# Pool and convolution-gate panels as seven block products, with weight sums made by DMA

## The chip, the cores and the metric

The kernel runs on one core of a Trainium2 chip. The metric is the device time of one launch in microseconds; it is compared as the median of several runs, and one more execution is recorded by the hardware profiler.

## The reference

The reference is one decoder block on 512 tokens of width 1024 in float32, with 256 memory tokens. Cut to what the change touches:

```python
h = rmsnorm(x, g_mix)
proj = h @ w_in                                   # 512 x 1024 @ 1024 x 6144
za, zb, zc, zg = jnp.split(proj, IN_SPLITS, axis=-1)
ya = chunked_spatial_gating(gelu(za)) @ w_branch_a
yb = short_gated_conv(zb, b_conv) @ w_branch_b    # gb * conv3(gc * xin)
yc = multiscale_pool(zc, c_wg, c_scale) @ w_branch_c
gates = jax.nn.sigmoid(zg.reshape(nb, s, 3, D_MODEL) + b_gate)
x = x + (gates[:,:,0]*ya + gates[:,:,1]*yb + gates[:,:,2]*yc) @ w_o
x = x + cross_attention(x, mem)                   # keys and values from rmsnorm(mem) @ w_xkv
x = x + swiglu_ffn(x)
```

A final RMSNorm follows. Two pieces of `proj`, each 512 columns wide, are the subject: `gb` (the gate that multiplies the convolution) and `zc` (the input of the pool).

## The kernel before

**Panels.** All weights come as panels of 128 partitions x 2048 float32 (1 MB), numbered in the order of use: V0 = 0 (values), K0 = 4 (keys), SV0 = 8, SU0 = 10, GC0 = 12, XI0 = 14, PC0 = 16 (pool, two panels), GB0 = 18 (convolution gate, two panels), GA0 = 20 (six times two gate panels and one branch panel), and then the output projection, the attention and the feed-forward part. SyncE (SP) loads panel n into slot n % 2 of `raw` as soon as the low part of panel n - 2 is made (`lo_ready`), in order, one queue.

**Splits.** Every float32 product is three matmuls (`mm3`, lines 1614 to 1616): high by high, high by low, low by high. For each panel ACT copies `raw` to a rounded high part (`split_hi`), and DVE subtracts it to get the low part (`split_lo`). Both are in-order engines and walk through a hand-written list of such steps, interleaved with the arithmetic of the stage.

**Full and seven-product panels.** `fm_panel` (line 1629) computes 256 output features for 512 tokens with 48 matmuls of 512 columns. The twelve gate panels from GA0 on use `gate_seven` (line 1794): the panel is cut into 2 x 2 blocks, and seven block products with sums of weight blocks (S1 to S4) and sums of token blocks (T1 to T4, `gth`/`gtl`) replace eight. It has 84 matmuls of 256 columns. Between its products ACT keeps partial results (`keep`: s1, s5, u2, u3 into `gsnap`), and DVE adds them at the end (`gate_add`). The weight sums are four DVE additions in `gate_prep` (line 1163), in place in `raw`; `gate_pair_hi` and `gate_prep_lo` then split the sums into high and low parts.

**The order around the change.** TensorE runs XI0 (two panels), sixteen transposes, PC0 and PC0+1, GB0 and GB0+1 as full panels, four pool products (three matmuls each), then GA0 and GA0+1 in seven products and the first branch panel. ACT copies the pool input to `zp`; DVE computes the running means from it (`pool_window`) and multiplies the convolution by the gate. POOL makes the weight sums of the feed-forward output, `fo_sums`, in DRAM with accumulating DMAs, beginning when `mixed` is reached; each step waits until the one before has landed.

**The first products.** `v_half(0)` computes two value panels whose pieces arrive one after the other; each step waits for the high and low parts of both operands. Ahead of it `WARM` = 14 products of ones run, 28 matmuls in the profile.

Of the kernel before, what the change touches and what calls it, by code (L numbers as in the profile page):

```python
# [28 lines left out]
P = 128  # L29
D = 1024  # L30
S = 512
# [12 lines left out]
NG = 12  # L44
# [7 lines left out]
WARM = 14  # L52
# [32 lines left out]
def build(nc, first_in, weights, fo_in, x_in, xt_in, memt_in, cols_in, sgu_in, wg_in, ln_g_in, ln_b_in, gf_in, out):  # L85
    base = -(-nc.sbuf_base // 32) * 32

    kv_store = nc.dram_tensor("kv_store", (4, P, KT * M), F32).ap()
    fo_sums = nc.dram_tensor("fo_sums", (NP, P, 4, S), F32).ap()
# [25 lines left out]
    gsnap = at("gsnap", 200, [2, S])  # L115
    hole = lambda t: t[:, 0:4, S // 2:S].rearrange("p k (b f) -> p b k f", b=2)
# [85 lines left out]
    with ExitStack() as ctx:  # L202
# [29 lines left out]
        def landing(n):  # L232
            return 16 * (n // SLOTS - K0 // SLOTS + 1)
# [46 lines left out]
        fo_made = sem("fo_made")  # L280
# [46 lines left out]
        def _(sp):  # L327
# [12 lines left out]
            with sp.Fori(K0 // 2 + 1, FO0 // 2) as i:  # L340
                for s in range(SLOTS):
                    sp.wait_ge(lo_ready, 2 * i + (s - 1))
                    sp.dma_start(raw[:, s, :], weights[2 * i + (s - 2)]).then_inc(landed[s], 16)
            for q in range(2 * NP + 1):
# [6 lines left out]
                if q == 0:  # L351
                    sp.wait_ge(fo_made, 16 * 3 * NP)
# [18 lines left out]
        def _(pool):  # L371
# [22 lines left out]

            pool.wait_ge(panel_done, K0 + 1)
# [14 lines left out]
            made = 0  # L410
            for step in range(NP + 2):
                if step < NP:
                    pool.dma_start(fo_sums[step], fo_in[step, :, 0:4 * S].rearrange("p (b c) -> p b c", b=4)).then_inc(fo_made, 16)
                    made += 16
                if 1 <= step <= NP:
                    q = step - 1
                    pool.dma_start(fo_sums[q, :, 1:4, :], fo_in[q, :, 3 * S:6 * S].rearrange("p (b c) -> p b c", b=3),
                                   accum_op=ALU.add).then_inc(fo_made, 16)
                    made += 16
                if step >= 2:  # L420
                    q = step - 2
                    pool.dma_start(fo_sums[q, :, 0:4:2, :], fo_sums[q, :, 1:4:2, :], accum_op=ALU.add).then_inc(fo_made, 16)
                    made += 16
                pool.wait_ge(fo_made, made)
# [29 lines left out]
        def _(act):  # L454
# [130 lines left out]
            split_hi(XI0 + 2)  # L585

            for g in range(BT):
                act.wait_ge(a_fm, g + 1)
                copy(acth[:, g, :], bank[4 + g][:]).then_inc(acth_ready, 1)
            def gate_sigmoid(h, j, t):  # L590
                b, half = h // 2, h % 2
                i = 4 * half + 2 * j + t
                act.wait_ge(gate_sum if t == 0 else up_sum, 2 * h + j + 1)
# [4 lines left out]
                nc.scalar.activation(sig[:, 2 * j + t, :], bank[2 * j + t][:], ACT.Sigmoid,  # L598
                                     bias=col(C_BG + 8 * b + i)).then_inc(low_read, 1)

            def gate_panel_of(h, j):

                return GA0 + 3 * h + j, 2 * h + j
# [9 lines left out]
            def gate_pair_hi(n, i, pair):  # L613
                act.wait_ge(s2_ready if pair == 0 else s4_ready, i + 1)
# [3 lines left out]
            def keep(i, j, which):  # L618

                left, right = bank[2 * j], bank[2 * j + 1]  # L620
                done, kept, dst, src = {
                    "s1": (p1_done, s1_kept, gsnap[:, 0, 0:Q], right[:, Q:S]),
                    "s5": (p5_done, s5_kept, gsnap[:, 1, Q:S], left[:, Q:S]),
                    "u2": (p6_done, u2_kept, gsnap[:, 0, Q:S], right[:, Q:S]),
                    "u3": (p7_done, u3_kept, gsnap[:, 1, 0:Q], right[:, Q:S])}[which]
                act.wait_ge(done, i + 1)
# [15 lines left out]
            for n in range(2):  # L642
                split_hi(PC0 + n + 1)
                if n:
                    pool_hi(0)
                    pool_hi(1)
                for t in range(2):
# [1504 lines left out]
```

## Time and profile before

| what | us |
|---|---|
| median of 3 runs (lowest, highest) | 884.63 (884.46, 885.09) |
| profiled execution | 884.56 |
| its span (first to last instruction) | 882.7 |
| TensorE busy | 874.2 |
| DVE busy | 649.0 |
| ACT busy | 420.0 |
| POOL busy | 78.4 |

The span is what the profiler's records cover; the profiled execution's own time is a little longer. Busy time counts each engine by itself, and matmuls overlap, so that their mean durations don't add up to their busy time; stages are read from the times at which they start. A weight panel's "us to landing" is counted from its issue on the queue.

### The profile page before, as it was taken

The numbers are of one execution on the slowest core, as the hardware profiler recorded it, in microseconds if no ns is written. First come the engines' busy times: TensorE is split into PE (matmuls) and PEld (weight loads), VectorE is DVE, ScalarE is ACT, GpSimd is POOL, SyncE is SP. The second block draws the span as 40 slices with busy tenths as digits, with TensorE's granted clock in tenths as the row PEclk, the third lists the DMA queues.
The fourth block names the chain that finished last, engine by engine and source line by source line (L and its number), as shares of the span: only waits on it lengthen the run. The fifth ranks groups of instructions, "written<-read, shape, count | busy, mean of one in ns | idle before, by whom it ended". The sixth has DMA issues, their size and how long they took to land.

```text
span 882.7 us, 13301 instructions
## 1 busy us (share of the span) xinstructions
PE 874.2 (99%) x5232; PEld 781.9 (89%) x5232; DVE 649.0 (74%) x825; ACT 420.0 (48%) x629; POOL 78.4 (9%) x89
## 2 busy tenths in 40 slices
PE   9999999999999999999999999999999999999997
PEld 7998888889999999988888888899999999988885
DVE  5684667688676687765456465898888888789877
ACT  6655432345444544533234332455554455467555
POOL 0101011112110000014200045000000000000001
PEclk9999999999999999999999999999999999999999
DMA  9956449999987423472221123214222332376522
GB/s 341 371 186 237 145 176 223 261 212 288 244 217 180 143 78 114 144 333 97 96 96 48 48 68 123 96 49 141 97 95 95 101 123 97 107 242 236 191 95 96
DMA packets 26012, 139.64 MB, mean 158 GB/s; under 512 B 2800, under 2 KB 2928, under 8 KB 13936
## 3 DMA queue, kind: packets, MB, share of 16 engines
q1 hardware_dynamic: 17728, 101.85, 32.1%
q0 software_dynamic: 6064, 25.17, 12.6%
q10 hardware_dynamic: 2176, 12.00, 3.6%
q8 instruction: 31, 0.51, 0.2%
q14 instruction: 13, 0.11, 0.0%
HBM read 132.72 MB, written 29.88 MB: 184 GB/s over the span
## 4 chain that ended last, share of the span: by engine, by line
PE 90%; DVE 5%; ACT 2%; issue 1%; DMA 1%; ACTq 0%; POOLq 0%; POOL 0%; DVEq 0%
PE psum L1614 30%; PE psum L1616 29%; PE psum L1615 29%; DMA pack<-first 1%; DVE tl L980 1%; DVE wl L980 1%; ACT wh L455 0%; DVE fol L980 0%; PE psum L1666 0%; PE psum L1866 0%; DVE w7l L980 0%; DVE hn L1401 0%; PE psum L1993 0%; DVE gt L1391 0%; ACT th L455 0%
## 5 line engine op out<-in xcount | busy, mean ns | idle before, releaser
L1614 PE MATMUL psum<-th,w7h 128*128 128x256 f32 x504 | 142.7, 283 | 0.3 <-ACT snap L455 0.3
L1615 PE MATMUL psum<-tl,w7h 128*128 128x256 f32 x504 | 142.6, 283 | 0.0
L1616 PE MATMUL psum<-th,w7l 128*128 128x256 f32 x504 | 142.6, 283 | 0.0
L980 DVE TENSOR_TENSOR wl<-raw,wh 128x2048 fp32r<-128x2048 f32 (+1 forms) x44 | 89.2, 2039 | 49.2 <-ACT wh L455 49.1
L1614 PEld LDWEIGHTS psum<-th,w7h 128*128 128x128 f32 x504 | 96.7, 192 | 0.5 <-issue 0.5
L1615 PEld LDWEIGHTS psum<-tl,w7h 128*128 128x128 f32 x504 | 96.8, 192 | 0.0
L1616 PEld LDWEIGHTS psum<-th,w7l 128*128 128x128 f32 x504 | 96.8, 192 | 0.0
L455 ACT ACTIVATE wh<-raw 128x2048 fp32r<-128x2048 f32 (+1 forms) x44 | 73.1, 1675 | 21.1 <-PE psum L1616 19.8
L1614 PE MATMUL psum<-hh,wh 128*128 128x512 f32 x192 | 75.0, 391 | 0.0
L1616 PE MATMUL psum<-hh,wl 128*128 128x512 f32 x192 | 74.7, 389 | 0.0
L1615 PE MATMUL psum<-hl,wh 128*128 128x512 f32 x192 | 74.7, 389 | 0.0
L455 ACT ACTIVATE snap<-psum 128x256 f32<-128x256 f32 x72 | 27.7, 384 | 84.1 <-PE psum L1616 80.8
L455 ACT ACTIVATE blk<-raw 128x1024 fp32r<-128x1024 f32 (+1 forms) x36 | 42.4, 1198 | 49.9 <-DVE raw L1171 25.4
L1614 PE MATMUL psum<-foh,hsh 128*128 128x512 f32 x156 | 61.5, 394 | 0.6 <-DVE fol L980 0.5
L1616 PE MATMUL psum<-foh,hsl 128*128 128x512 f32 x156 | 60.8, 390 | 0.0
L1615 PE MATMUL psum<-fol,hsh 128*128 128x512 f32 x156 | 60.8, 390 | 0.0
L1614 PE MATMUL psum<-gth,blk 128*128 128x256 f32 x192 | 54.4, 284 | 0.0
L1615 PE MATMUL psum<-gtl,blk 128*128 128x256 f32 x192 | 54.3, 283 | 0.0
L980 DVE TENSOR_TENSOR w7l<-psum,w7h 128x1024 fp32r<-128x1024 f32 x36 | 43.7, 1216 | 0.0
L1616 PEld LDWEIGHTS psum<-hh,wl 128*128 128x128 f32 x192 | 36.0, 188 | 7.5
L1615 PEld LDWEIGHTS psum<-hl,wh 128*128 128x128 f32 x192 | 36.1, 188 | 7.4
L1614 PEld LDWEIGHTS psum<-hh,wh 128*128 128x128 f32 x192 | 36.1, 188 | 7.3
(280 smaller groups left out, 2282.7 us busy)
## 6 DMA issues: line engine op xcount, KB each, us to landing
raw<-weights SPq DMA_DIRECT2D x68, 1024.0 KB, 4.8
fo_sums<-fo POOLq DMA_DIRECT2D x10, 1024.0 KB, 5.9
fo_sums<-fo POOLq DMA_DIRECT2D x10, 768.0 KB, 10.3
fo_sums<-fo_sums POOLq DMA_DIRECT2D x10, 512.0 KB, 13.6
raw<-fo_sums SPq DMA_DIRECT2D x10, 512.0 KB, 4.7
more<-fo_sums SPq DMA_DIRECT2D x10, 512.0 KB, 4.7
more<-fo SPq DMA_DIRECT2D x6, 512.0 KB, 3.7
pack<-first SPq DMA_DIRECT2D x3, 768.0 KB, 8.2
```

The costliest lines, as they stand in the source:

```text
L455: copy = lambda o, i, **kw: nc.scalar.activation(o, i, ACT.Copy, **kw)
L980: return V.tensor_tensor(dst, v, f32(hi), ALU.subtract)
L1614: nc.tensor.matmul(dst, lh, rh, start=start, stop=False, **kw)
L1615: nc.tensor.matmul(dst, lh, rl, start=False, stop=False, **kw)
L1616: return nc.tensor.matmul(dst, ll, rh, start=False, stop=stop, **kw)
```

## The change

The pool and convolution-gate panels (16 to 19) are laid out in blocks and computed in seven products. Their partial results are kept in `gsnap_first`. These four panels and GA0 and GA0+1 use a new order of the seven, `seven_plain_first`, which begins with the three products that need no weight sums. The weight sums of these six panels are not made by DVE: POOL makes them in DRAM, two panels at a time, with copies and accumulating DMAs, at most two in flight. SP loads such a panel's blocks 1 to 3 first, and then the four sums into the same slot. The signs of token and weight sums change, so that every weight sum is an addition; the second output of a panel comes out negated, and is turned by a scale of -1 where it is read. The making of `fo_sums` begins after panel GA0+1. `v_half(0)` issues the high products of a step before it waits for the low parts, and `WARM` is 12. ACT's and DVE's lists are reordered. Counters of semaphores shift accordingly.

```diff
-NG = 12
+NG = 16
+ND = 6
+NM = NG - ND
-WARM = 14
+WARM = 12
+    w_sums = nc.dram_tensor("w_sums", (ND, P, 4, 4 * P), F32).ap()
+    gsnap_first = at("gsnap_first", 140, [2, S])
+        made_for = (112, 112, 192, 192, 240, 240)
@@ sync
+            def load_sums(n):
+                sp.wait_ge(lo_a, n - PC0 + 1)
+                sp.wait_ge(sums_made, made_for[n - PC0])
+                sp.dma_start(raw[:, n % SLOTS, :], w_sums[n - PC0].rearrange("p b f -> p (b f)")).then_inc(landed[n % SLOTS], 16)
+            for n in range(K0 + 2, GA0 + 4):
+                if n == GA0 + 2:
+                    load_sums(n - 1)
+                sp.wait_ge(lo_ready, n - 1)
+                cs = slice(4 * P, PANEL) if by_transfer(n) else slice(0, PANEL)
+                sp.dma_start(raw[:, n % SLOTS, cs], weights[n - 2, :, cs]).then_inc(landed[n % SLOTS], 16)
+                if PC0 <= n - 1 < GA0 + 1:
+                    load_sums(n - 1)
@@ gpsimd
+            def together(*transfers):
+                pool.wait_ge(sums_made, made[0])
+                for part, g in transfers:
+                    two, src = w_sums[2 * g:2 * g + 2], weights[PC0 + 2 * g - 2:PC0 + 2 * g]
+                    if part == "copy":
+                        transfer(two, src.rearrange("n p (b f) -> n p b f", b=4))
+                    elif part == "s1":
+                        transfer(two[:, :, 0, :], src[:, :, 4 * P:8 * P], accum_op=ALU.add)
...
+            pool.wait_ge(panel_done, SV0)
+            together(("copy", 0))
+            together(("s1", 0), ("s3", 0))
+            together(("s2", 0), ("copy", 1))
             for t in range(TT):
                 pool.wait_ge(var_ready, t + 3)
                 rsqrt(small(RS + t), small(VR + t), 1).then_inc(rstd_ready, 1)
+            together(("s4", 0), ("s1", 1))
+            together(("s3", 1))
+            together(("s2", 1), ("copy", 2))
+            together(("s4", 1), ("s1", 2))
+            together(("s3", 2))
+            together(("s2", 2))
+            together(("s4", 2))
             pool.wait_ge(mixed, 4)
             pool.dma_start(wgr[:], wg_in).then_inc(wg_here, 16)
+            pool.wait_ge(sums_made, made[0])
+            pool.wait_ge(panel_done, GA0 + 2)
@@ scalar
+            act.wait_ge(gtl_ready, 4)
+            gate_plain_hi(PC0, 0)
+            pair_hi(PC0, 0)
+            gate_plain_hi(PC0 + 1, 1)
+            for g in range(BT):
+                act.wait_ge(a_fm, g + 1)
+                copy(acth[:, g, :], bank[4 + g][:]).then_inc(acth_ready, 1)
             keep(0, 0, "s1")
             keep(0, 0, "s5")
             keep(0, 0, "u2")
+            pair_hi(PC0 + 1, 1)
             keep(0, 0, "u3")
+            gate_plain_hi(GB0, 2)
+            keep(1, 1, "s1")
+            padded(0)
+            keep(1, 1, "s5")
+            keep(1, 1, "u2")
+            pair_hi(GB0, 2)
+            keep(1, 1, "u3")
+            pool_hi(0)
+            pool_hi(1)
+            gate_plain_hi(GB0 + 1, 3)
+            keep(2, 0, "s1")
...
@@ vector
+            gate_prep(PC0 + 1, 1)
             for g in range(BT):
                 dve.wait_ge(acth_ready, g + 1)
                 lo(actl[:, g, :], bank[4 + g][:], acth[:, g, :]).then_inc(actl_ready, 1)
+            add_left(PC0, 0, 0)
+            gate_prep_lo(PC0 + 1, 1)
+            add_right(PC0, 0, 0)
+            gate_prep(GB0, 2)
+            pool_window(0)
+            pool_window(1)
+            add_left(PC0 + 1, 1, 1)
+            gate_prep_lo(GB0, 2)
+            add_right(PC0 + 1, 1, 1)
+            gate_prep(GB0 + 1, 3)
...
+            add_left(GA0, 4, 0)
+            gate_prep_lo(GA0 + 1, 5)
+            add_right(GA0, 4, 0)
             for g in range(4):
                 dve.wait_ge(acth_ready, 2 * BT + g + 1)
                 lo(actl[:, 2 * BT + g, :], bank[4 + g][:], acth[:, 2 * BT + g, :]).then_inc(high_read, 1)
+            split_lo(GA0 + 2)
+            for i in range(4):
+                conv_lo(i)
@@ tensor
+            def v_step(k):
+                pe.wait_ge(memh_ready, k + 1)
+                pe.wait_ge(*of_piece(k, piece_hi, hi_ready))
+                # memh x wh for both mt
+                pe.wait_ge(meml_ready, k + 1)
+                # meml x wh
+                pe.wait_ge(*of_piece(k, piece_lo, lo_ready))
+                # memh x wl
...
+            def seven_plain_first(n, i, j, free):
+                left, right = bank[2 * j], bank[2 * j + 1]
+                pe.wait_ge(lo_a, i + 1)
+                pe.wait_ge(*free)
+                gate_product(right[:, Q:S], n, 0, 1, "B11", start=True).then_inc(p1_done, 1)
+                gate_product(left[:, 0:Q], n, 0, 2, "B21", start=True)
+                pe.wait_ge(s1_kept, i + 1)
+                gate_product(right[:, 0:Q], n, 0, 0, "T4")
+                pe.wait_ge(lo_s13, i + 1)
+                gate_product(left[:, Q:S], n, 1, 0, "T1").then_inc(p5_done, 1)
+                gate_product(right[:, Q:S], n, 1, 1, "T2").then_inc(p6_done, 1)
+                pe.wait_ge(lo_ready, n + 1)
+                pe.wait_ge(s5_kept, i + 1)
+                gate_product(left[:, Q:S], n, 2, 1, "B22").then_inc(p3_done, 1)
+                pe.wait_ge(u2_kept, i + 1)
+                gate_product(right[:, Q:S], n, 2, 0, "T3").then_inc(panel_done, 1)
             for n in range(2):
-                fm_panel(PC0 + n, h_hi, h_lo, first_tile, [(cx_ready, 2 * n + t + 1) for t in range(2)])
+                seven_plain_first(PC0 + n, n, n, (cx_ready, 2 * n + 2))
             for n in range(2):
-                fm_panel(GB0 + n, h_hi, h_lo, first_tile, [(zp_ready, 2 * n + t + 1) for t in range(2)])
+                seven_plain_first(GB0 + n, 2 + n, n, (zp_ready, 2 * n + 2))
```

In `keep`, s1 of a panel also waits until DVE has added the left sum of the panel before (`gate_sum`). DVE's `gate_prep` makes only the low part of blocks 1 to 3 (`lo_a`) for the six panels.

## Rows read from the trace of the kernel before

**Rows 1.** Page part 1, busy time by engine; then the waits of PE.

```profile
PE 874.2 (99%) x5232; PEld 781.9 (89%) x5232; DVE 649.0 (74%) x825; ACT 420.0 (48%) x629; POOL 78.4 (9%) x89
...
PE psum L1614 <- DVE actl L980: 0.2, 1, 0.2
```

**Rows 2.** Stages: start:end, length, busy (xinstructions) PE, PEld, DVE, ACT, POOL; clock, DMA share, GB/s.

```profile
146.26:189.87 43.61, 43.61 (x195) 36.13 (x193) 30.98 (x46) 15.80 (x19) 6.86 (x9) 1.00 0.91 233
...
189.87:193.05 3.18, 3.00 (x13) 2.17 (x12) 2.41 (x5) 0.85 (x2) 0.00 (x0) 1.00 1.13 172
...
193.05:213.47 20.42, 20.42 (x170) 20.19 (x168) 19.20 (x24) 13.20 (x21) 2.28 (x3) 1.00 1.01 255
...
224.48:244.63 20.15, 20.15 (x169) 20.15 (x168) 12.24 (x13) 9.19 (x14) 2.29 (x3) 1.00 1.00 262
```

**Rows 3.** Timeline, the start: start us, duration, engine, line, op, out<-in.

```profile
9.50 0.47 PE L1614 MATMUL psum<-wh,memh 128*128 128x512 f32 x1 [0.67 <-DVE wl L980]
...
8.02 0.62 ACT L455 ACTIVATE wh<-pack 128x512 fp32r<-128x512 f32 x1
...
8.66 0.69 DVE L980 TENSOR_TENSOR wl<-pack,wh 128x512 fp32r<-128x512 f32 x1
...
28.57 1.03 POOL L388 TENSOR_TENSOR sm<-sm,cst 128x4 f32<-128x4 f32 x1 [26.85 <-DVE sm L1018]
...
29.99 1.05 PE L1666 MATMUL psum<-ident,sm 128*128 128x128 f32 x8
...
52.05 2.35 DVE L980 TENSOR_TENSOR wl<-raw,wh 128x1024 fp32r<-128x1024 f32 x2
```

**Rows 4.** Timeline of ACT and DVE around the first gate panels.

```profile
193.97 1.47 ACT L455 ACTIVATE blk<-raw 128x1536 fp32r<-128x1536 f32 x1
...
200.91 2.00 ACT L455 ACTIVATE blk<-raw 128x1024 fp32r<-128x1024 f32 x2
...
205.06 0.39 ACT L455 ACTIVATE gsnap<-psum 128x256 f32<-128x256 f32 x1 [2.15 <-DVE psum L1186]
...
144.85 0.69 DVE L1146 TENSOR_TENSOR yp<-psum,cv 128x512 f32<-128x512 f32 x1 [2.71 <-PE psum L1616]
...
146.88 0.75 DVE L1151 SCALAR_TENSOR_TENSOR cv<-yp,cols,cv 128x512 f32<-128x512 f32 x1
...
196.79 1.75 DVE L980 TENSOR_TENSOR blk<-raw,blk 128x1536 fp32r<-128x1536 f32 x1
...
203.13 1.22 DVE L980 TENSOR_TENSOR hl<-raw,blk 128x1024 fp32r<-128x1024 f32 x1
...
204.27 0.69 DVE L1186 TENSOR_TENSOR psum<-psum,gsnap 128x512 f32<-128x512 f32 x1
```

**Rows 5.** Loads issued at 152.5, 195.8, 271.9, 265.0: KB, us to landing.

```profile
raw<-weights SPq DMA_DIRECT2D x1, 1024.0 KB, 4.8
...
raw<-weights SPq DMA_DIRECT2D x1, 1024.0 KB, 6.1
...
raw<-weights SPq DMA_DIRECT2D x1, 1024.0 KB, 6.5
...
raw<-weights SPq DMA_DIRECT2D x1, 1024.0 KB, 9.2
```

**Rows 6.** POOL's accumulation issued alone at 276; then the stretch of two whole groups.

```profile
fo_sums<-fo_sums POOLq DMA_DIRECT2D x1, 512.0 KB, 5.4
...
154.06:185.55 31.49, 31.49 (x140) 26.10 (x139) 20.85 (x32) 10.35 (x12) 4.56 (x6) 1.00 0.93 248
```

**Rows 7.** Windows before POOL's transfers begin.

```profile
55.00:77.00 22.00, 22.00 (x98) 18.20 (x97) 12.98 (x21) 11.41 (x18) 0.00 (x0) 1.00 0.40 144
...
77.00:92.00 15.00, 15.00 (x67) 12.39 (x67) 10.19 (x18) 7.97 (x17) 2.49 (x4) 1.00 0.90 349
...
92.00:123.80 31.80, 31.80 (x142) 26.34 (x141) 16.17 (x16) 12.79 (x14) 0.51 (x1) 1.00 0.29 100
```

**Rows 8.** Timeline of POOL, the LayerNorm rsqrts.

```profile
85.01 2.49 POOL L388 TENSOR_TENSOR sm<-sm,cst 128x1 f32<-128x1 f32 x4 [38.76 <-DVE sm L1098]
```

More of the change, by code:

```diff
@@ L393, in _, with transfer @@
             rsqrt(small(RM, MT), small(VM, MT), MT).then_inc(rstd_ready, 1)
+            made = [0]
+            def transfer(dst, src, **kw):
+                made[0] += 16
+                pool.dma_start(dst, src, **kw).then_inc(sums_made, 16)
+            def together(*transfers):
[6 more added lines that the diff above has]
+                        transfer(two[:, :, 0, :], src[:, :, 4 * P:8 * P], accum_op=ALU.add)
+                    elif part == "s3":
+                        transfer(two[:, :, 2, :], src[:, :, 0:4 * P], accum_op=ALU.add)
+                    elif part == "s2":
+                        transfer(two[:, :, 1, :], two[:, :, 2, :], accum_op=ALU.add)
+                    else:
+                        transfer(two[:, :, 3, :], two[:, :, 1, :], accum_op=ALU.add)
             pool.wait_ge(panel_done, K0 + 1)
@@ L613, in gate_pair_hi @@
             def gate_pair_hi(n, i, pair):
-                act.wait_ge(s2_ready if pair == 0 else s4_ready, i + 1)
+                if by_transfer(n):
+                    act.wait_ge(landed[n % SLOTS], landing(n, sums=True))
+                else:
+                    act.wait_ge(s2_ready if pair == 0 else s4_ready, i - ND + 1)
                 copy(gate_hi[n % 2][1 + pair], raw_blocks(n % SLOTS)[:, 2 * pair:2 * pair + 2]).then_inc(
@@ L620, in keep @@
                 left, right = bank[2 * j], bank[2 * j + 1]
+                held = gsnap_first if i < 4 else gsnap
                 done, kept, dst, src = {
[L622 to L626, printed above, removed]
+                    "s1": (p1_done, s1_kept, held[:, 0, 0:Q], right[:, Q:S]),
+                    "s5": (p5_done, s5_kept, held[:, 1, Q:S], left[:, Q:S]),
+                    "u2": (p6_done, u2_kept, held[:, 0, Q:S], right[:, Q:S]),
+                    "u3": (p7_done, u3_kept, held[:, 1, 0:Q], right[:, Q:S])}[which]
+                if which == "u3" and i < ND:
+                    act.wait_ge(panel_done, PC0 + i + 1)
+                else:
+                    act.wait_ge(done, i + 1 - (ND if which == "u3" else 0))
                 if i and which == "s1":
@@ L681, in _ @@
                 copy(acth[:, 2 * BT + g, :], bank[4 + g][:]).then_inc(acth_ready, 1)
-            keep(1, 1, "u3")
+            pair_hi(GA0 + 1, 5)
+            keep(4, 0, "u3")
+            keep(5, 1, "s1")
+            split_hi(GA0 + 2)
+            keep(5, 1, "s5")
+            keep(5, 1, "u2")
+            keep(5, 1, "u3")
             for t in range(2):
@@ L1137, in _, with add_right, gate_add @@
+            def add_right(n, i, j):
+                held = gsnap_first if i < 4 else gsnap
+                dve.wait_ge(panel_done, n + 1)
+                dve.wait_ge(u3_kept, i + 1)
+                V.tensor_tensor(bank[2 * j + 1], bank[2 * j + 1], held[:, 1, :], ALU.add).then_inc(up_sum, 1)
+            def gate_add(n, i, j):
+                add_left(n, i, j)
+                add_right(n, i, j)
             for n in range(2):
-                split_lo(XI0 + n + 1)
                 if n == 0:
+                    split_lo(XI0 + 1)
@@ L1752, in _, with gate_product @@
                 ins.then_inc(a_fm, 1)
+            tokens = {"B11": lambda k: (hh[:, k, 0:Q], hl[:, k, 0:Q]),
+                      "B21": lambda k: (hh[:, 4 + k, 0:Q], hl[:, 4 + k, 0:Q]),
+                      "B22": lambda k: (hh[:, 4 + k, Q:S], hl[:, 4 + k, Q:S])}
+            for q, name in enumerate(("T1", "T3", "T2", "T4")):
+                tokens[name] = lambda k, q=q: (gth[:, q, k, :], gtl[:, q, k, :])
+            def gate_product(dst, n, group, which, name, start=False):
+                hi, low = gate_hi[n % 2][group], gate_lo[n % 2][group]
+                for k in range(4):
+                    ins = mm3(dst, hi[:, which, k, :], low[:, which, k, :], *tokens[name](k),
+                              start and k == 0, k == 3, skip_group_check=True)
+                return ins
```

314 lines of the change are left out of this document (164 added, 150 removed).

## The prediction

> **What bounds the kernel now.** I read the page's table of busy time first: TensorE is busy for 874.2 of 882.7 us, 99%, and the list of its waits adds up to under 3 us, one of them the 0.2 us on `actl` [rows 1]. A microsecond of matmuls saved is a microsecond of time only if the weight splits of ScalarE (ACT) and VectorE (DVE) and the loads behind them keep up. So I cut the stretch that the change rewrites into stages. The four pool and convolution-gate panels take 43.61 us, the pool products 3.18, the first two gate panels 20.42, and the first branch panel begins at 213.47. Two later gate panels, without waits, take 20.15 [rows 2]. The granted clock is 1.00 (2.4 GHz) in all. The profiled execution took 884.56 us, 1.86 more than its span and 0.07 under the median of 884.63; I sum against 884.56.
>
> **Matmuls removed.** A panel in seven products has 84 matmuls of 256 columns, 20.15/2 = 10.08 us, against 43.61/4 = 10.90 now [rows 2]. Four panels: 43.61 − 40.30 = 3.3 us less. Two small terms go with them. The pool products are 12 matmuls of 512 columns, at 10.90/48 = 0.227 each 2.7 us; they take 3.18 because the last one waits for DVE's `actl` [rows 1]. With the pool windows moved ahead, I count 0.4 saved (0 to 0.5). The first gate pair gives back 20.42 − 20.15 = 0.3. The branch panel could begin 4.0 us earlier if nothing waits.
>
> **The start.** Now the first value product waits until the low parts are there; afterwards the high products go first. Step 2 of TensorE starts at 9.50, released by DVE's `wl` of 8.66; ACT's `wh` of 8.02 ends at 8.64 [rows 3]. So step 2 can start 0.8 us earlier; the shorter warm-up (24 instead of 28 matmuls in 6.12 us, so 0.9 us less) lets step 1 go before it. But at the end of this phase the `spread` product, now at 29.99, needs POOL's rstd, 28.57 + 1.03 = 29.60. What follows needs DVE's halves of `wl`, and SV0 (54.8 now) needs DVE's `wl`, 52.05 + 2.35 = 54.40 [rows 3]. These are paced by loads and by DVE. I count 0.4 saved, bounds 0 (DVE and ACT slip) and 0.8 (they follow).
>
> **The new loop.** For panels 16 to 21 (PC0 to GA0+1) DVE's four sums per panel (0.7 each) are gone; the sums come by a second load into the same slot. SP issues it once DVE has written `lo_a`, and on its in-order queue the next panel's load stands behind it. I worked the three queues forward with these durations [rows 4]: ACT copies 1536 columns in 1.4, a pair of 1024 in 1.9, 512 in 0.5, 256 in 0.3 (0.4 with the signal); DVE's low parts take 1.7 for 1536 and 1.14 for 1024, an add 0.6, one convolution tile 2.8.
>
> From the landing of one panel's sums to the issue of the next's: first copy 1.1, two low parts 2.3, add 0.6, next `lo_a` 1.8, together 5.8. With landing time L the loop is L + 5.8, against 10.08 of TensorE: it keeps pace for L of 4.3 at most. A load in quiet lands in 4.8; where POOL's transfers are in flight 6.1, 6.5 and 9.2 [rows 5].
>
> At L = 4.8 everywhere: sums of 16 issued at 137.3 (XI0 ends at 133.9, then 1.5 and 1.8), landed 142.1; of 17, 142.1 + 1.1 + 2.3 + 2.8 + 1.8 = 150.0, landed 154.8. ACT then needs 1.9 + 0.3 + 1.4 + 0.4 = 4.0 until `s1_kept`, 158.8, and the third product of panel 17 can start at 146.26 + 10.08 + 2.88 = 159.2: no wait. Panel 18: issued 160.6, landed 165.4, and with two pool copies more 5.0 to `s1_kept`: 170.4 against 169.3, wait 1.05. Panel 19: 0.24. Before the branch panel DVE has, one behind the other, two low parts, an add, four low parts, a 2048 split and four convolution low parts, 9.9 us after panel 21's first sum is copied: wait 0.66. Together 1.95, so net 4.0 − 1.95 + 0.4 = 2.45 saved: 882.1 (rival A).
>
> **Are the transfers quiet then?** POOL makes the sums in ten steps, each waiting for the one before. From the trace: a transfer has about 1.9 us in which the DMA engines do not work for it (a 512 KB accumulation alone lands in 5.4). Two whole groups lie in 154.06 to 185.55, at a share of 0.93: 29.3 us of engine time; two weight loads take 6.2 of it (three alone take 0.29 x 31.8 = 9.2 [rows 7], so 3.1 each), 23.1 remain for 2 MB copied and 2.5 MB accumulated; with the copy at 3.1 per MB that is 6.8 per MB accumulated [rows 6]. The steps: copy of 2 MB 8.1, two accumulations 8.8, one with a copy 11.6, 8.8, 5.4, 11.6, 8.8, 5.4, 5.4, 5.4: 79 us. They begin when the keys are through, at 55: 134 with nothing else on the engines. Other traffic from 55 to 137 is 8.8 + 13.5 + 9.2 (share times length [rows 7]) + 3 = 34.5 us of engine time, of which perhaps ten fit into the idle parts. So the chain ends near 155 to 165, and the sums of 16 to 18 are loaded beside it. The counts they wait for are in time: 112 by about 110 for 137, 192 by about 150 for 160, 240 by about 165 for 182.
>
> The Trainium skill, page "DMA: Bandwidth & Descriptors", section "Anatomy of one DMA — SWDGE (gpsimd) path", fits a GpSimd transfer as 2.0 us plus its bytes at 436 GB/s. By it a 512 KB accumulation takes 3.2 us (an estimate), the chain about 49 us, and it would be over near 115 even with the loads; the row of 5.4 [rows 6] speaks against it. The time would then be rival A's.
>
> **Sum.** I take L = 6.5, 6.0 and 5.5 for panels 16, 17, 18 (single accumulations in flight: nearest are the 6.1 and 6.5) and 4.8 after. Behind the first pair copy that waits for a landing stand, on ACT, the second, `u3`, the next panel's plain copy and its `s1`; on DVE the adds and the next `lo_a`. Panel 16: landed 143.8; ACT pair 1.9, plain 1.4, four copies 2.0, keep 0.3: 149.4 against 149.15, wait 0.3. Panel 17: issued 143.8 + 7.9, landed 157.7, kept 161.7 against 159.5: 2.2. Panel 18: landed 169.0, kept 174.0 against 171.8: 2.2. Then 0.24 and 0.66. Waits 5.6; net 4.0 − 5.6 + 0.4 = 1.2 lost: **885.8**.
>
> **What costs nothing.** POOL's LayerNorm rsqrts now stand behind two waits for sums, over at about 80, and are wanted at 85.0 [rows 8]; if late, they hold DVE's norm, ACT's `svh` and the weight split behind it, whose low part ends at 96.05 in the timeline, 2.3 us before GC0 wants it at 98.35: the cost from then on is one to one. The weight loads from 60 to 126 have 6 us and more before ACT wants them, more than the 4.4 that a busy queue adds. The output-weight sums move from 124 to about 211 and end near 370, for use after 745; sum_squares first wants POOL at 387. `wgr` lands near 165, wanted after 170. `gsnap_first`, signs and `scale=-1.0` change operands, not counts. The two adds more per early panel are in the loop above.
>
> **Rivals.**
> A, quiet (0.30): the chain is over by about 135, or its steps leave the engines free when SP needs them, and L stays 4.8. For it: the load of 152 landed in 4.8 just before a new group, beside the end of the old [rows 5]. Against: the engine time above. 882.1, from 880.2 (no waits) to 883.2.
> B, forecast (0.45): 885.8, own range 883.0 to 888.6.
> C, crowded (0.17): two accumulations beside the sums of 16, L = 9.2, then 7.2 and 7.2: waits 2.9 + 3.3 + 3.9 + 0.9 = 11.0, so 884.56 − 4.4 + 11.0 = 891.2. It decides when step seven is still running at 137. With 9.2 for all six panels, worked the same way, the waits are 23 and the time 903; I leave that end out of the range. Rival A takes C's place if step seven is over by then.
> D (0.08): the panels save 3.3, but gains at the start and the pool products fail and a moved transfer (the X reload at 371, landed at 381, wanted at 386) loses a little: 884.6.
> That the seven products don't replace the full ones is excluded: 84 matmuls for 48 stand in the code.
>
> **How the numbers follow.** 0.2% is 1.8 us, about what a measurement can tell. Faster (under 882.8): 0.26 of A, 0.03 of B. Same (to 886.4): 0.04 of A, 0.22 of B, 0.07 of D. Slower: 0.20 of B, 0.17 of C, 0.01 of D. So 0.29, 0.33, 0.38. The range from 881.4 to 889.8 leaves out the best of A and most of C.
>
> **What would show it.** TensorE has 5232 + 4 x 36 − 4 = 5372 matmuls, its busy time is about 3.5 us lower. The second load of each panel lands in 5 to 7 us at 137 to 170, under 5 after. TensorE waits at the third product of panels 17 and 18 for ACT's `gsnap_first`, about 2 us each, and about 0.7 for `actl` before the branch panel. POOL's last sum is issued between 150 and 165. I am wrong if the sums land in under 5 us (then A), if TensorE waits for something else than s1, or if the start gives other than 0.4.

## The result and the profile after

| what | before | after |
|---|---|---|
| median, us | 884.61 | 893.16 |
| lowest, highest | 884.46, 885.09 (4 runs) | 890.79, 898.51 (4 runs) |
| profiled execution | 884.56 | 894.29 |
| its span | 882.7 | 892.5 |
| TensorE busy | 874.2 | 872.6 |

The change makes the kernel slower: ratio 1.0103, 95% interval 1.0082 to 1.0124. The forecast was 885.8 with a range of 881.4 to 889.8; the time lies outside it. What follows is read from the one profiled execution after; the other three, among them the one of 898.51, have no trace.

The first part of the page after, beside [rows 1]. The matmuls are the 5372 that were counted, and their busy time fell by 1.6 us, while the span grew by 9.8.

```profile
PE 872.6 (98%) x5372; PEld 786.7 (88%) x5372; DVE 655.9 (73%) x833; ACT 430.5 (48%) x653; POOL 92.3 (10%) x104
```

The waits of PE after (line waited for: us in all, times, longest). At the top stands the wait that was named in the prediction, for ACT's copy of the first partial result, but with 6.9 us in one place. These figures count the idle time of the engine; measured from start to start the same places cost 0.15 more each.

```profile
PE psum L1748 <- ACT gsnap_first L511: 9.7, 3, 6.9
PE psum L1848 <- POOL cst L406: 1.1, 1, 1.1
PE psum L1813 <- ACT wh L511: 0.8, 2, 0.6
PE psum L1800 <- POOL sm L413: 0.7, 1, 0.7
PE psum L1748 <- DVE actl L1075: 0.5, 1, 0.5
```

The timeline of PE at the third product of panels 16, 17 and 18 (T4, which needs s1 kept), and at the branch panel:

```profile
150.83 0.39 PE L1748 MATMUL psum<-gth,blk 128*128 128x256 f32 x1 [1.38 <-ACT gsnap_first L511]
...
168.02 0.58 PE L1748 MATMUL psum<-gth,blk 128*128 128x256 f32 x1 [6.85 <-ACT gsnap_first L511]
...
181.59 0.39 PE L1748 MATMUL psum<-gth,blk 128*128 128x256 f32 x1 [1.45 <-ACT gsnap_first L511]
...
222.73 0.47 PE L1748 MATMUL psum<-acth,wh 128*128 128x512 f32 x1 [0.51 <-DVE actl L1075]
```

The same stages as in [rows 2]: the four panels (43.61 before), the pool products (3.18), the first two gate panels (20.42).

```profile
146.34:199.16 52.82, 43.14 (x339) 42.38 (x338) 39.80 (x58) 24.15 (x40) 3.23 (x4) 0.94 0.69 184
199.16:201.91 2.75, 2.75 (x14) 2.26 (x13) 2.75 (x4) 2.75 (x4) 0.00 (x0) 1.00 0.02 6
201.91:222.73 20.82, 20.32 (x170) 20.14 (x168) 18.06 (x24) 11.43 (x21) 0.00 (x0) 1.00 0.47 166
```

The clock column says 0.94 for the first stage. In windows of 4 us around the long wait it stands apart:

```profile
158.00:162.00 4.00, 3.17 (x27) 2.96 (x25) 0.00 (x0) 0.00 (x0) 0.00 (x0) 1.00 0.96 300
162.00:166.00 4.00, 0.00 (x0) 0.00 (x0) 0.86 (x1) 1.95 (x3) 0.88 (x1) 0.91 0.12 19
166.00:170.00 4.00, 1.98 (x9) 1.98 (x10) 4.00 (x5) 2.94 (x6) 0.00 (x0) 0.50 1.04 212
170.00:174.00 4.00, 4.00 (x28) 4.00 (x28) 3.73 (x10) 0.39 (x1) 1.48 (x2) 0.74 0.89 357
174.00:178.00 4.00, 4.00 (x36) 4.00 (x35) 1.44 (x4) 1.81 (x3) 0.00 (x0) 1.00 0.93 162
```

TensorE stood still for 6.85 us, and came back at a granted clock of 0.50, which is 1.2 GHz; only from 174 on is it 2.4 GHz throughout. From the start of the third product of panel 17 (168.02) to the start of the same product of panel 18 (181.59, less the wait of 1.61) lie 84 matmuls in 11.96 us instead of 10.08: 1.9 us for the slow clock. (The Trainium skill, page "TensorE: Matmul & The Clock Gate", section "Part 1: The HAM clock gate", tells of these two levels and of the fall after idleness; the rows agree.)

So the account of the 9.26 us by which the first branch panel starts later (222.73 against 213.47) is: panels −3.3, pool products −0.4, gate pair −0.3, all before panel 16 +0.1 (it starts at 146.34 against 146.26); waits at the third product 1.5 + 7.0 + 1.6 = 10.1; wait for `actl` 0.7; slow clock 1.9; five gaps of 0.08 to 0.11 us each, together 0.5. That is 9.3. Behind it nothing is won or lost: the last matmul starts at 885.94 against 876.69, still 9.25 later. The remaining 0.6 of the 9.8 us by which the span grew lies in the landing of the output.

What ACT waited for, before it could keep s1, was a landing. First the issues on SP's queue (the second loads of panels 16, 17 and 18 on L355), then POOL's chain:

```profile
137.45 0.33 SPq L355 DMA_DIRECT2D raw<-w_sums  x1
...
153.22 0.33 SPq L355 DMA_DIRECT2D raw<-w_sums  x1
...
169.79 0.33 SPq L355 DMA_DIRECT2D raw<-w_sums  x1
```

```profile
55.18 0.52 POOL L425 DMA_DIRECT2D w_sums<-weights  x1 [8.04 <-PE psum L1750]
...
79.35 0.87 POOL L425 DMA_DIRECT2D w_sums<-w_sums  x1 [10.98 <-DMA w_sums<-weights]
...
103.42 0.93 POOL L425 DMA_DIRECT2D w_sums<-w_sums  x1 [15.40 <-DMA w_sums<-weights]
...
140.11 0.88 POOL L425 DMA_DIRECT2D w_sums<-w_sums  x1 [12.46 <-DMA w_sums<-weights]
...
152.40 0.87 POOL L425 DMA_DIRECT2D w_sums<-weights  x1 [10.50 <-DMA w_sums<-weights]
164.14 0.88 POOL L425 DMA_DIRECT2D w_sums<-w_sums  x1 [10.87 <-DMA w_sums<-weights]
170.60 0.87 POOL L425 DMA_DIRECT2D w_sums<-w_sums  x1 [5.58 <-DMA w_sums<-w_sums]
```

And the landings of the transfers issued at 137.45, 153.22 and 169.79, and of POOL's at 118.00 and 152.40 (KB, us to landing):

```profile
raw<-w_sums SPq DMA_DIRECT2D x1, 1024.0 KB, 7.7
...
raw<-w_sums SPq DMA_DIRECT2D x1, 1024.0 KB, 10.8
...
raw<-w_sums SPq DMA_DIRECT2D x1, 1024.0 KB, 6.8
...
w_sums<-weights POOLq DMA_DIRECT2D x1, 512.0 KB, 8.0
...
w_sums<-weights POOLq DMA_DIRECT2D x1, 512.0 KB, 11.5
```

The load at 153.22 and the accumulation at 152.40 are in flight together and take 10.8 and 11.5 us. The load at 137.45 shares its flight with step seven of the chain, issued at 140.11, and the load at 169.79 with step ten, issued at 170.60. ACT's timeline shows what follows: it waits 8.22 us for the landing of panel 17's sums, and then needs the list of the prediction (the pair of copies, `u3`, the next panel's plain copy, s1) until s1 is kept.

```profile
164.05 2.00 ACT L511 ACTIVATE blk<-raw 128x1024 fp32r<-128x1024 f32 x2 [8.22 <-DMA raw<-w_sums]
165.96 0.36 ACT L511 ACTIVATE gsnap_first<-psum 128x256 f32<-128x256 f32 x1
166.22 1.47 ACT L511 ACTIVATE blk<-raw 128x1536 fp32r<-128x1536 f32 x1
167.60 0.37 ACT L511 ACTIVATE gsnap_first<-psum 128x256 f32<-128x256 f32 x1
```

### The profile page after: what moved, and what is told of

Same layout as the page of the kernel before. It is cut to its first block, busy times and chain, and to the rows that moved or that the text cites. A ratio compares the mean times of both kernels' runs of the same rounds, so it can differ in the third digit from the quotient of the medians.

```text
span 892.5 us, 13634 instructions
## 1 busy us (share of the span) xinstructions
PE 872.6 (98%) x5372; PEld 786.7 (88%) x5372; DVE 655.9 (73%) x833; ACT 430.5 (48%) x653; POOL 92.3 (10%) x104
## 4 chain that ended last, share of the span: by engine, by line
PE 82%; DVE 6%; DMA 5%; ACT 4%; issue 2%; SPq 0%; POOL 0%; POOLq 0%; ACTq 0%; DVEq 0%
PE psum L1748 27%; PE psum L1750 27%; PE psum L1749 27%; DMA raw<-w_sums 3%; DMA xt<-xt 2%; DVE blk L1075 1%; ACT blk L511 1%; DVE wl L1075 1%; DVE tl L1075 1%; DVE actl L1075 1%; DVE fol L1075 0%; PE psum L1800 0%; ACT wh L511 0%; PE psum L2037 0%; ACT xt L555 0%
## 5 line engine op out<-in xcount | busy, mean ns | idle before, releaser
L511 ACT ACTIVATE blk<-raw 128x1024 fp32r<-128x1024 f32 (+1 forms) x48 | 56.3, 1198 | 72.8 <-PE psum L1750 29.8
L1748 PE MATMUL psum<-gth,blk 128*128 128x256 f32 x256 | 73.8, 288 | 9.7 <-ACT gsnap_first L511 9.7
L1749 PE MATMUL psum<-gtl,blk 128*128 128x256 f32 x256 | 73.2, 286 | 0.0
L1748 PEld LDWEIGHTS psum<-gth,blk 128*128 128x128 f32 x256 | 50.0, 195 | 10.4 <-ACT gsnap_first L511 10.4
L1075 DVE TENSOR_TENSOR blk<-raw,blk 128x1536 fp32r<-128x1536 f32 (+1 forms) x32 | 47.0, 1488 | 15.9 <-ACT blk L511 15.8
L1748 PE MATMUL psum<-hh,blk 128*128 128x256 f32 x192 | 54.4, 283 | 0.0
L1749 PE MATMUL psum<-hl,blk 128*128 128x256 f32 x192 | 54.3, 283 | 0.0
L1748 PE MATMUL psum<-hh,wh 128*128 128x512 f32 x128 | 50.0, 391 | 0.0
L1749 PEld LDWEIGHTS psum<-gtl,blk 128*128 128x128 f32 x256 | 50.0, 195 | 0.0
L1750 PE MATMUL psum<-hh,wl 128*128 128x512 f32 x128 | 49.8, 389 | 0.0
```

The costliest lines, as they stand in the source:

```text
L511: copy = lambda o, i, **kw: nc.scalar.activation(o, i, ACT.Copy, **kw)
L1075: return V.tensor_tensor(dst, v, f32(hi), ALU.subtract)
L1748: nc.tensor.matmul(dst, lh, rh, start=start, stop=False, **kw)
L1749: nc.tensor.matmul(dst, lh, rl, start=False, stop=False, **kw)
L1750: return nc.tensor.matmul(dst, ll, rh, start=False, stop=stop, **kw)
```

## The experiments

The theory after the comparison: the panels and their loop do what was worked out, and what went wrong is that POOL's chain is still in flight when SP loads the sums, so that these land late. Its rivals are that the second load is slow by itself, that it is slow because it reads the tensor that POOL writes, that the order of ACT's list sets the waits, and that the start does.

**The chain cut to two groups.** The sums of panels 20 and 21 aren't made; their second loads read plain weights in place of the sums.

```diff
-            together(("s2", 1), ("copy", 2))
-            together(("s4", 1), ("s1", 2))
-            together(("s3", 2))
-            together(("s2", 2))
-            together(("s4", 2))
+            together(("s2", 1))
+            together(("s4", 1))
@@ load_sums
-                sp.dma_start(raw[:, n % SLOTS, :], w_sums[n - PC0]...)
+                src = w_sums[n - PC0]... if n < GA0 else weights[n - 2]
+                sp.dma_start(raw[:, n % SLOTS, :], src)...
```

> POOL makes the sums of panels 16 to 19 only (two groups instead of three); panels 20 and 21 load their weight blocks a second time in place of the sums, so their results are not the reference's. Loads, waits and matmuls are the same. Theory 1 (the sums land late because POOL's chain of transfers is still on the DMA engines after 137 us): the chain is over near 140, the sums of 16, 17 and 18 land in about 5.5, 4.8 and 4.8 us instead of 7.7, 10.8 and 6.8, TensorE's waits for s1 fall from 10.2 to about 2 us, and the time is 884 to 885.5 (893.2 less 8 to 9). Theory 2 (the order of ACT's and DVE's lists sets the waits, whatever the loads do): waits stay near 10 us and the time near 893.

Measured: 885.56 (883.34 to 886.93, 10 runs), ratio 1.0007 (0.9998 to 1.0017). POOL's last step is issued at 135.12. The second loads of panels 16, 17 and 18, issued at 137.4, 153.3 and 163.7:

```profile
raw<-w_sums SPq DMA_DIRECT2D x1, 1024.0 KB, 7.8
...
raw<-w_sums SPq DMA_DIRECT2D x1, 1024.0 KB, 4.7
...
raw<-w_sums SPq DMA_DIRECT2D x1, 1024.0 KB, 5.2
```

Its waits for s1, and the window behind the longest of them:

```profile
PE psum L1746 <- ACT gsnap_first L509: 3.9, 3, 1.7
```

```profile
174.00:178.00 4.00, 4.00 (x33) 4.00 (x34) 3.83 (x6) 1.82 (x4) 0.00 (x0) 1.00 0.83 284
```

Without transfers beside them the loads of 17 and 18 land in 4.7 and 5.2, the waits shrink from 10.1 to 4.5 (1.6, 0.9, 1.9, 0.15 from start to start), the clock stays at 1.00, and 7.6 of the 8.5 us are back. Panel 16's load, which meets the end of the shorter chain, still takes 7.8.

**No chain.** No sums are made, the second loads read plain weights in place of the sums, and nothing else is altered.

```diff
-            together(("copy", 0))
-            together(("s1", 0), ("s3", 0))
...
-            together(("s4", 2))
-                sp.wait_ge(sums_made, made_for[n - PC0])
-                sp.dma_start(raw[:, n % SLOTS, :], w_sums[n - PC0]...)
+                sp.dma_start(raw[:, n % SLOTS, :], weights[n - 2])...
```

> POOL makes no weight sums at all; the second load of each of the six panels reads its plain blocks from weights (results are not the reference's). Everything else is the changed kernel. Theory 1 (the loss is the second loads landing late beside the chain): all landings 4.8 us, waits about 1.0 for s1 at panel 18, 0.2 at 19 and 0.7 before the branch panel, time 882.1 to 883 (the price of my rival A less the start's 0.4). Theory 2 (the lists of ACT and DVE or the start hold more back than I counted): 885 or more.

Measured: 882.96, ratio 0.9988 (0.9973 to 1.0003); the four runs are 886.01, 882.71, 883.21, 882.64. This is the floor of the change as it stands: with sums for nothing its median is 1.8 us (0.2%) under the kernel before, and the interval reaches past 1, so that even this gain isn't clear of the noise. The second load of panel 16 takes 6.2 us here with no transfer of POOL at all; those of 17 to 19 take 4.7, 5.3 and 4.8. The profiled run is the one of 886.01. Its trace shows waits of 0.9 and 2.0 us at panels 17 and 18, and behind the second a stretch in which the granted clock is 0.58; that this sets it above the other three, which have no trace, is likely but not shown.

```profile
170.00:174.00 4.00, 2.19 (x18) 1.99 (x18) 3.34 (x4) 3.95 (x7) 0.00 (x0) 0.99 0.45 159
174.00:178.00 4.00, 4.00 (x23) 4.00 (x23) 3.79 (x9) 0.38 (x1) 0.00 (x0) 0.58 0.82 290
178.00:182.00 4.00, 4.00 (x35) 4.00 (x35) 3.17 (x6) 2.79 (x5) 0.00 (x0) 1.00 0.05 16
```

There are 23 matmuls in 4 us where 35 are the rule. The wait of 1.9 in the kernel with two groups was not followed by such a stretch.

**The chain kept, the second loads from another tensor.** POOL makes all the sums, but the loads read plain weights.

```diff
-                sp.dma_start(raw[:, n % SLOTS, :], w_sums[n - PC0]...)
+                sp.dma_start(raw[:, n % SLOTS, :], weights[n - 2])...
```

> All of POOL's chain and every wait stays, but the second load of each of the six panels reads the panel's plain blocks from weights in DRAM instead of w_sums (results are not the reference's). Theory 1 (the loads share the DMA engines with the chain, whatever they read): landings as before, about 7.7, 10.8 and 6.8 us, time 891 to 895. Theory 3 (the loads are slow because they read the tensor that the accumulations are writing): landings of 5 to 6.5 us, waits 2 to 4 us less each at panels 16 to 18, time 885 to 888.

Measured: 895.26, ratio 1.0125 (1.0097 to 1.0152). The second loads of panels 16 to 19 land in 7.6, 5.4, 8.5 and 7.6, the waits are 1.4, 1.6, 5.1 and 1.2. The loss stays whole, and loads that read only weights are slow too, so that the tensor they read isn't the cause.

Its place has changed, though: panel 17's load took 5.4 where it took 10.8 in the changed kernel. In both, POOL's accumulation was issued just ahead of it, 0.16 us before here (152.88 and 153.04) and 0.82 before there. The packets show the difference; q0 is POOL's queue and q1 is SP's. In the changed kernel from 154 to 158 the accumulation's packets ran and the load's hardly did:

```profile
q0 software_dynamic: 129, 0.26, 94.3%
q1 hardware_dynamic: 8, 0.07, 4.6%
```

With the loads from weights, from 153.5 to 157, the load's ran first:

```profile
q1 hardware_dynamic: 126, 0.98, 80.9%
q0 software_dynamic: 3, 0.01, 0.9%
```

So a load beside an accumulation lands late when the accumulation's packets run ahead of its own, and nearly as in quiet when its own run first.

**The start alone**, in the kernel before.

```diff
-WARM = 14
+WARM = 12
+            def v_step(k):
...
                     if half == 0:
-                        pe.wait_ge(meml_ready, k + 1)
-                        pe.wait_ge(*of_piece(k, piece_lo, lo_ready))
-                    elif k % 4 == 0:
+                        v_step(k)
+                        continue
+                    if k % 4 == 0:
```

> The kernel before with only the new order of the first value products and the shorter warm-up. Theory from the trace after (the first key stage waits for POOL's rstd and DVE's low parts, so the start gives back all it gains): 884.5, within 0.2 of before. Rival (my term of the prediction): 0.4 us faster, 884.2.

Measured: 884.55 (11 runs), ratio 0.9997 (0.9988 to 1.0006). The start gives nothing that can be measured, though the interval doesn't exclude the 0.4 either. In the trace SV0 starts at 54.50 instead of 54.80, and the first branch panel at 213.20 instead of 213.47, so that in this execution the start gave 0.3 and kept it.

**The sums by DVE**, as before the change, for all six panels; one load for each panel, `fo_sums` at its old place.

```diff
-ND = 6
+ND = 0
-                return PC0 <= n < GA0 + 2
+                return False
-            def load_sums(n):
...
-            together(("copy", 0))
...
```

> All matmuls, keeps and lists of the changed kernel, but DVE makes the sums of the six panels in place as it does for the later ones, no second loads and no w_sums; fo_sums begins at mixed again. If the DMA round trip is the whole loss: the waits for s1 go, DVE's additions of 2.9 us a panel come on top of its list, time 882 to 885. If DVE's list is the next bound (six panels of 8.7 us with 22 us of pool, convolution and low parts beside them in 60 us of matmuls): waits of 5 to 10 us for the sums of late panels and before the branch panel, 887 to 892. I hold the second likelier.

Measured: 893.9, ratio 1.0105 (1.009 to 1.0121). DVE becomes the bound: busy for 74.82 of 78 us (146 to 224), against 53.35 of 68 before. TensorE waits 3.7 and 0.9 for s1 and 2.9 and 1.0 for `actl`, and the clock is 0.93 over the stretch.

```profile
146.00:224.00 78.00, 70.07 (x527) 68.30 (x526) 74.82 (x105) 38.91 (x63) 11.41 (x15) 0.93 0.92 235
```

The same stage of the kernel before:

```profile
146.00:214.00 68.00, 67.82 (x379) 59.24 (x378) 53.35 (x76) 30.34 (x41) 9.14 (x12) 1.00 0.95 235
```

So these panels gain nothing unless the sums are taken off DVE, and POOL's chain costs as much as it takes off.

**ACT keeps s1 first**, ahead of the plain copy and the four `acth` copies, for panels 16 to 19; the first two of the four places are shown.

```diff
             gate_plain_hi(PC0 + 1, 1)
+            keep(0, 0, "s1")
             for g in range(BT):
                 ...
-            keep(0, 0, "s1")
-            gate_plain_hi(GB0, 2)
             keep(1, 1, "s1")
+            gate_plain_hi(GB0, 2)
...
```

> The changed kernel with s1 of panels 16 to 19 kept before the 1.4 us (panels 17 to 19) or 2.0 us (panel 16) of ACT copies that stood in front of it. If a late landing reaches TensorE by ACT's list (pair copies, u3, plain copy, s1): each of the waits shrinks by up to its copy, 1.5 to 0 at panel 16, 7.0 to 5.6 at 17, 1.6 to 0.3 at 18, so 888.8 to 890.5 for 893.2. If DVE's low parts of the sums are what TensorE would wait for next, the wait moves to lo_s13 and the time stays within 1 us of 893.

Measured: 893.89, ratio 1.0108 (1.009 to 1.0127). The wait at panel 16 is gone, but the loads of 17 and 18 land in 11.0 and 9.1, the waits there are 6.6 and 4.2, and `actl` costs 1.2. (The trace is of the slowest of the four runs, 897.04.) From the landing to the third product it now takes 2.6 us at panel 17 instead of 4.0, and 3.7 at panel 18 instead of 5.0: the order does what was expected on that path, but the time isn't won, since panel 18's load lands 2.3 us later than in the changed kernel. The late landings set the loss, whatever ACT's order.

**The same, and the chain starts at 46.5** instead of 55.

```diff
-            pool.wait_ge(panel_done, SV0)
             together(("copy", 0))
```

> As the last, and POOL's chain starts right after its mask step at about 47 us instead of 55. If the end of the chain sets how late the sums land: it ends some 8 us earlier, near 168, the single steps that met the loads of 17 and 18 are shifted, and the time is 1 to 4 us below the last, 885 to 889. If the loads of the key panels suffer first, TensorE waits for wh or wl at 40 to 60 us and the gain is lost.

Measured: 891.07 (888.47 to 896.38), ratio 1.008 (1.0047 to 1.0112). The second loads now land in 4.9, 7.2 and 5.1, and the waits for s1 fall to 2.6 in all. But the first seven-product panel starts at 151.50 instead of 146.34. The loads issued at 49, 55 and 61 (panels 9 to 11) land in 8.0, 6.9 and 9.2 instead of 4.8, 4.8 and 8.2, without a wait of TensorE. It pays the 5.2 us at panel 11, near 91: a wait for DVE's `wl`, and in the window around it PE is busy for 4.78 of 8 us at a clock of 0.84.

```profile
PE psum L1747 <- DVE wl L1074: 3.2, 1, 3.2
```

```profile
86.00:94.00 8.00, 4.78 (x16) 3.51 (x15) 5.54 (x10) 5.51 (x11) 2.91 (x5) 0.84 1.01 420
```

Panel 11 had landed at 70. It was late because ACT, before it splits this panel, issues the four stores of `kv_store`, and the issue of the second took 5.49 us (the first line) where it took 0.68 in the changed kernel (the second line):

```profile
77.43 5.49 ACTq L608 DMA_DIRECT2D kv_store<-kl  x1
```

```profile
77.37 0.68 ACTq L609 DMA_DIRECT2D kv_store<-kl  x1
```

ACT's split of the panel started at 86.71 instead of 81.16. POOL's copy of 2 MB had been issued at 71.72 and was in flight (it took 13.8 us); in the changed kernel it is issued at 79.91, behind the stores. That the copy holds up ACT's issue is inferred from these times; no run separates it.

**Four panels by POOL, two by DVE**, with s1 kept first, at first with the early start. Waits and counts that go with `ND` shift.

```diff
-ND = 6
+ND = 4
-                return PC0 <= n < GA0 + 2
+                return PC0 <= n < PC0 + ND
```

> As the last, but POOL makes the sums of panels 16 to 19 only and DVE those of 20 and 21, as before (a complete kernel). The chain ends near 132, before the first second load at 137. By theory 1 the sums of 16 to 18 land in 4.8 to 5.2 and cause no wait; DVE's list gets 5.8 us longer, so a wait of 1 to 4 us near panel 20 or before the branch panel. 882.5 to 886: the only one of the four complete kernels here that may beat the kernel before.

Measured: 893.08, ratio 1.0102 (1.0087 to 1.0117). TensorE waits 2.8 us for `kl` near 66 (the load issued at 49 took 11.2 us here, and ACT's and DVE's lists stood behind it), and the clock is 0.57 from 66 to 70. The first seven-product panel starts at 151.04. It has second loads in 4.9, 5.1, 4.8 and 4.7, and waits for `actl` of 3.4 and 1.3.

The same with the start at 55:

```diff
+            pool.wait_ge(panel_done, SV0)
             together(("copy", 0))
```

> e8_four_panels with the chain's first step back behind SV0 (at 55 instead of 46.5): sums of panels 16 to 19 by POOL, of 20 and 21 by DVE, complete. Theory (e8's early start cost the 4.7 us that its first seven-product panel was late, DVE's list the rest): that panel starts at 146.3, the time is 893.1 - 4.7 = 888.4 (887 to 889.8), with the 3.4 us wait on actl in the pool products still there. Rival (all of e8's loss is DVE's list, the early 4.7 is made good later): 892 or more.

Measured: 890.37, ratio 1.0062 (1.0045 to 1.0078). The first such panel starts at 146.20 again, and 2.7 us are back, not the 4.7 expected: the wait for s1 at panel 18 is 2.0 where it was under 0.7. The largest wait left is for DVE's list, 3.4 us in the pool products as with the early start, after which the clock falls again:

```profile
190.00:194.00 4.00, 1.24 (x6) 0.68 (x4) 3.83 (x9) 1.36 (x2) 0.00 (x0) 1.00 0.00 0
194.00:198.00 4.00, 3.55 (x15) 3.18 (x16) 4.00 (x6) 3.84 (x6) 0.00 (x0) 0.70 0.02 4
```

**The chain paced**: the same bytes, but each of the last five transfers waits until a second load has landed (the last three wait for the same one), and the sums of panels 16 to 19 are finished first.

```diff
-            together(("s2", 1), ("copy", 2))
...
-            together(("s4", 2))
+            together(("s2", 1))
+            together(("s4", 1))
...
+            for n, part in ((0, "copy"), (1, "s1"), (2, "s3"), (2, "s2"), (2, "s4")):
+                pool.wait_ge(landed[(PC0 + n) % SLOTS], landing(PC0 + n, sums=True))
+                together((part, 2))
```

> The changed kernel, complete, with POOL's last five transfers held back: the sums of panels 16 to 19 are made first (nine steps' worth is over near 137), then the copy of group 2 starts only when the second load of panel 16 has landed, its s1 when that of panel 17 has, and s3, s2, s4 (one by one) when that of panel 18 has; wgr is loaded before them. The same bytes move, only not beside SP's second loads. Theory (the landings of the second loads are what costs): they land in 4.8 to 6 us, the waits at the third product are 1.5 or less each as in e1_two_groups (1.59, 0.91, 1.86, 0.15), the branch panel starts near 215 and the time is 885 (884 to 887). Rival (the volume of POOL's chain costs wherever it lies, or the loads are slowed by something else than the transfers beside them): the waits stay at 6 us or more in sum and the time is 890 or more.

Measured: 898.76 (896.44 to 900.45), ratio 1.016 (1.0146 to 1.0174), the slowest of all. The theory as I had put it fell: the second loads do land earlier, in 5.4 and 6.2 at panels 17 and 18 (7.2 at 19), but the transfers now lie beside the first loads of the next panels. Issued at 147.6 and 173.0, these take 7.5 and 7.8, where they took 4.1 with nothing beside them (in the kernels with two groups and without a chain) and 5.3 in the changed kernel. The first of them:

```profile
raw<-weights SPq DMA_DIRECT2D x1, 768.0 KB, 7.5
```

SP's queue is in order, and that load stands ahead of the next second load. And the chain, spread out, ends near 194.5, so that the sums of panel 20 come late:

```profile
PE psum L1748 <- ACT gsnap_first L511: 5.5, 4, 2.7
PE psum L1748 <- ACT gsnap L511: 4.2, 1, 4.2
```

The four waits for s1 are 0.65, 1.6, 2.8 and 1.0; together with the 4.2 that is as much as the waits of the changed kernel, and the clock falls twice, to 0.72 behind the wait of 2.8 (174 to 178) and to 0.63 and 0.52 behind the one of 4.2 (202 to 210). The first branch panel starts at 224.87, 2.1 later than in the changed kernel.

**The paced chain, with s1 kept first** as above:

> The paced chain of e9_paced, and on ACT the s1 copy of each early panel ahead of the plain and the acth copies. Theory: where the landing is quiet this order takes away the 1.5 us at panel 16 and leaves about 1 at panels 17 and 18: 0.5 to 1.5 us under e9_paced, 884 (882.5 to 885.5), at the kernel before or a little under it. Rival (the order only moves the wait on, as it did in e6_keep_first): equal to e9_paced within 0.5.

Measured: 897.5, ratio 1.0146 (1.013 to 1.0161): 1.3 us under the median without the reordering (the runs of the two overlap), which is the size expected of the order, and far above the expected time, with 1.2, 2.8 and 1.7 for s1 and 4.6 for panel 20.

No kernel of these that makes all the sums beats the kernel before. Seven products for panels 16 and 17 alone were not tried.

## Why the prediction was wrong

**The step that failed** is the landing time L of the second loads, and behind it the length of POOL's chain. I took 6.5, 6.0 and 5.5 for panels 16, 17 and 18, by the nearest landings of before [rows 5]; they took 7.7, 10.8 and 6.8. The rest of the loop was right, as the measured L put into it shows: the sums of 17 landed at 153.22 + 10.8 = 164.0, plus the 4.0 of ACT's list is 168.0, and the product started at 168.02; the loop's 5.8 from landing to the next issue gives 169.8 (measured 169.79); 169.79 + 6.8 + 5.0 = 181.6 (measured 181.59). The prediction had 2.2 us of wait at panel 17, from an L of 6.0; the wait was 7.0. For panel 16 the 6.5 was hardly a charge for POOL at all, since that load takes 6.2 with no chain; in the changed kernel it took 7.7.

**Why L was too small.** The prediction had the ten steps at 79 us by themselves, and an end between 155 and 165. They took 124 us, from 55.2 to about 179.5 (the last one lands 8.9 after its issue at 170.60). Two terms were too low. The steps themselves: the copy takes 11.0 (I had 8.1), and an accumulation of 512 KB at 118.00, with no weight load in flight for most of its time, 8.0, where I had taken the 5.4 of a `fo_sums` step [rows 6] (later ones took 6.2 and 8.9). And the meeting of two transfers: the step issued at 79.35 lies beside the 4 MB of `kv_store` and takes 24.1 us until the next (I had 11.6 and shared out 24 us of delay over the whole chain). A sum of engine time treats the two as if one only waited for the other's bytes, and says nothing of whose packets run first, which is what set the 10.8. By the Trainium skill's fit on the page "DMA: Bandwidth & Descriptors", section "Anatomy of one DMA — SWDGE (gpsimd) path", the copy would take 6.8 us and such an accumulation 3.2 (estimates); the rows show 11.0 and 8.0.

**The rival that came nearest** is C: 891.2, with 11.0 us of waits. Its condition was that step seven is still running at 137; it was issued at 140.11, and even step eight, at 152.40, met a load. The waits came to 10.8. Its sum agrees better than its parts: it had 2.9, 3.3, 3.9 and 0.9 where 1.5, 7.0, 1.6, nothing at panel 19 and 0.7 for `actl` were measured, so the match of the sum is partly luck. I gave it 0.17, since I trusted the end of the chain; the kernel with two groups (885.6) and the one without a chain (883.0) show that the chain in flight makes the difference to 893.

**What no case had** is the clock: 1.9 us behind the wait of 6.85. C's price with it is 893.1.

**The start** was sized at 0.4 and gave 0.06 in the profiled execution: SV0 starts at 54.74 instead of 54.80. The `spread` product waited 0.69 for POOL's rstd, which starts at 28.67 and ends at 29.70. The start alone gave 0.30 at the same place, and the traces of the changed kernel's variants have SV0 anywhere from 54.61 to 55.15, so that the true size, between nothing and 0.4, can't be told from these runs.

**What held**: 5372 matmuls; 3.3 us for the four panels, 0.43 for the pool products (0.4), 0.27 for the gate pair (0.3: 20.82 less the 0.67 wait is 20.15); 0.67 for `actl` (0.66); the weight loads from 60 to 126, some of which took 8 to 15.6 us, without a wait of TensorE; POOL's rsqrts at 85.53. `fo_sums` ended at 409 instead of near 370, and POOL's sum of squares began then instead of at 387; it cost nothing, since the last matmul is late by the same 9.25 us as the branch panel.

**TensorE's busy time** fell by 1.6 instead of 3.5, since the matmuls at the low clock are longer; once the clock has moved, busy time isn't a measure of the work removed.

## What to carry to other kernels

When a buffer's load is taken into a loop twice, work out the landing time at which the loop just keeps pace (here 4.3 us against 4.7 at best), and allow, for every other transfer that can be in flight then, that its packets run ahead of the load's. Beside one, the loads here took from 1.1 to 2.3 times their time in quiet; a mean engine share doesn't show that. Moving the other transfers about only chose who paid: with a start at 46.5 ACT's issues and earlier loads, with the paced chain the first loads and panel 20, and with four panels DVE's list. Price a wait of several microseconds on TensorE with the slow clock behind it.

## What the runs showed of the hardware

- A load of 1 MB took 4.7 to 5.3 us with nothing beside it at panels 17 to 19. With an accumulation of 512 KB issued 0.82 and 1.20 us ahead of it, it took 10.8 and 11.0; issued 0.16 us ahead, 5.4. In the first case the accumulation's packets had 94.3% of the engines' time from 154 to 158 and the load's 4.6%, in the last the load's had 80.9% and the accumulation's 0.9% (153.5 to 157). What decides whose packets run first stays open.
- An accumulation of 512 KB took 8.0 us (118.00) and 6.2 us (164.14) with little beside it, and 11.5 beside the load that took 10.8. From 154 to 158, when it had the engines nearly alone, they moved 82 GB/s in all.
- A first load of 768 KB takes 4.1 us alone and 5.3 to 7.8 beside a POOL transfer.
- The issue of a 1 MB store on ACT's queue took 0.68 us in the changed kernel, and 5.49 us in the one where a 2 MB copy of POOL was in flight. ACT's engine was idle for 8.6 us over the four stores there, instead of 3.1.
- After 6.85 us of idleness TensorE's granted clock was 0.50, and matmuls took 0.58 us instead of 0.39 at first. In the window of 4 us behind a wait of 3.2 its mean was 0.70, behind one of 2.7 it was 0.72, and behind waits of 1.7 to 1.9 it was once 0.58 and twice 1.00. I can't say from these runs what decides it; it would explain why kernels with such waits scatter (888.5 to 896.4 in one of them) where the kernel before keeps within 884.2 and 885.7, but that was only argued.
